# Six different starting bytes for the split weight buffers, and a 64-column gate tile

## The chip, the cores and the metric

The kernel runs on one core of one Trainium2 chip. The metric is the time of one execution on the device in microseconds (us), the median of the runs shown. Lower is better. Throughout, L298 means line 298 of the kernel before.

## The reference

The program is a chain of four transformer layers on one sequence of 512 tokens with 1024 features, all in float32: a layer with a gated linear memory (mLSTM) and a pooling branch, a layer with index-selected attention, a layer with window attention, and a layer with sparse attention in three branches. The last two are each followed by a feed-forward network of width 2816. What matters here is what the layers have in common: a dense product of the 512 tokens with a weight matrix from HBM.

```
def even_layer(x, g_norm, w_in, conv_w, b_if, g_head, w_pool, s_pool, w_out):
    xn = rmsnorm(x, g_norm)
    p = xn @ w_in
    q, k, v, o, z_a, gates, u, z_b = _split(p, EVEN_SPLITS)
    ...
    gates = gates + b_if
    i_pre, f_pre = gates[..., :A_HEADS], gates[..., A_HEADS:]      # 4 + 4 columns
    ...
    return x + jnp.concatenate([y_a, y_b], axis=-1) @ w_out

def swiglu(h, w_gu, w_down):
    gate, up = jnp.split(h @ w_gu, 2, axis=-1)
    return (jax.nn.silu(gate) * up) @ w_down
```

The gate projection has eight output columns: four input gates and four forget gates.

## The kernel before, in words

**Weights.** All weights pass through one ring of 281 chunks. A chunk is 128 partitions by eight blocks of 128 float32 columns (4096 bytes a partition), except for eight chunks of six blocks. The ring has three slots (`SLOTS = 3`). SyncE issues the load of chunk c + 3 into `raw` once the low part of chunk c has been made. ScalarE copies `raw` to `whi`, rounded to fp32r (`split_high`, L2390), two chunks ahead of TensorE. VectorE writes `wlo = raw - whi` (`split_low`, L2399). TensorE waits for `wlo` of its chunk.

**Products.** `Dense.products` (L289 to L301) makes one output tile of 128 features by 512 tokens: for each block of 128 input features it issues three fp32r matmuls into the same PSUM bank, low weights by high activations, high by low, and high by high. The weights are the stationary operand (128x128, 512 bytes a partition), the activations move (128x512). `DenseRows` (L412 to L414) and `DownRows` (L598 to L600) do it the other way round: 128 tokens are stationary and 512 weight columns move. A chunk of eight blocks is 24 matmuls in all three classes; one of six blocks is 18.

**Addresses.** Memory is handed out by `sb`, in steps of 32 bytes a partition. `line_up` (L2234) moves the next buffer to byte 128 of a 512-byte row; it stands ahead of `raw`, ahead of `xs` (the activations, high and low) and ahead of nearly every other operand of a matmul. `raw`, `whi` and `wlo` are one tensor each with the three slots inside. As a slot is 4096 bytes, each slot, and each 512-byte block of a slot, begins at byte 128 of a row; so does each tile of `xs`.

**The gate tile.** `e_gates` (L2607) is a `Dense` of one tile. Its chunk holds 32 weight columns from 5120 on and 96 from 5124 on, so that the four input gates come out at PSUM partitions 0 to 3 and the four forget gates at 32 to 35. The two steps of its eviction (L2604) read those eight partitions and no others. Its products are 24 matmuls.

**Order.** Each engine runs its own list of stages in program order; the chunks fix the order of the dense products, and other work (attention, memory, norms) is placed beside them or between them by hand. Nothing in the order is computed from addresses.

Of the kernel before, what the change touches and what calls it, by code (L numbers as in the profile page):

```python
# [23 lines left out]
F32R = mybir.dt.float32r  # L24
# [4 lines left out]
P = 128  # L29
# [20 lines left out]
SLOTS = 3  # L50
# [3 lines left out]
ROW, ROW_AT = 512, 128  # L54
# [78 lines left out]
class Dense(Stage):  # L133
# [2 lines left out]

    def __init__(self, k, name, x_hi, x_lo, steps, ready=None, readers=None, scale=None, beside=(), spread=None, evicted=None,
                 between=None, evict_first=False, lead=0, trail=None, trail_from=0, trail_free=None, second=True, scale_at=0,
                 halved=(), beside_first=(), split_last=False):
        self.trail_from, self.trail_free, self.split_last = trail_from, trail_free, split_last  # L140
        evict_first = evict_first or split_last
        self.second, self.scale_at, self.halved, self.beside_first = second, scale_at, halved, beside_first
        self.between, self.evict_first, self.lead, self.trail = between, evict_first, lead, trail
        self.k, self.name, self.x_hi, self.x_lo, self.steps = k, name, x_hi, x_lo, steps
        self.ready, self.scale, self.beside, self.spread, self.evicted = ready, scale, beside, spread, evicted
        spec = k.plan[k.planned]
        assert spec["name"] == name, (spec["name"], name)
        k.planned += 1
        self.sizes, self.together, self.first, self.last = spec["sizes"], spec["together"], spec["first"], spec["last"]
        self.tiles = spec["tiles"]  # L150
        self.tile0, self.bank0 = len(k.tile_steps), len(k.banked)
        self.first_step = k.steps_planned
        for n in range(self.tiles):
            count = len(steps(n))
            k.tile_steps.append((k.steps_planned, 1 if readers is None else readers(n), spec["units"][n]))
            k.steps_planned += count
        self.take_banks()
# [130 lines left out]

    def products(self, pe, c, j, part, n, blocks):  # L289
        k, nc, chunk = self.k, self.k.nc, self.k.chunks[c]  # L290
        out = k.banks[:, self.bank(n), :]
        for b in blocks:
            kt = sum(self.sizes[:part]) + b
            if n <= (1 if self.lead else 0) and self.ready is not None:
                self.ready(pe, kt)
            at = b * self.together + j
            first, last = kt == 0, kt == sum(self.sizes) - 1
            nc.tensor.matmul(out, k.wlo[:, chunk.slot, at, :], self.x_hi(kt), start=first, stop=False)  # L298
            nc.tensor.matmul(out, k.whi[:, chunk.slot, at, :], self.x_lo(kt), start=False, stop=False)  # L299
            ins = nc.tensor.matmul(out, k.whi[:, chunk.slot, at, :], self.x_hi(kt), start=False, stop=last)  # L300
        return ins  # L301

    def trail_pe(self, pe):
# [51 lines left out]
class DenseRows(Dense):  # L355
# [38 lines left out]
    def on_pe(self, pe):  # L394
        k, nc = self.k, self.k.nc
        low, summed, evac = k.sig("weights_low"), k.sig("tile_summed"), k.sig("tile_steps")
        for c in range(self.first, self.last):
            slot = k.chunks[c].slot
            g, part = divmod(c - self.first, 4)
            high, rest = [w[:, slot].rearrange("p (k t) c -> p k (t c)", k=2) for w in (k.whi, k.wlo)]  # L400
            pe.wait_ge(low.sem, CREDIT + c + 1)
            for t in range(QT):
                if part == 0 and g > 0:
                    before, readers, _ = k.tile_steps[self.tile0 + QT * (g - 1) + t]
                    pe.wait_ge(evac.sem, CREDIT + before + readers)
                if part == 0 and g == 0 and self.between is not None:
                    self.between(pe, t)
                out = k.banks[:, 4 + t, :]
                r = slice(t * P, (t + 1) * P)
                for b in range(2):  # L410
                    kt = 2 * part + b
                    nc.tensor.matmul(out, self.x_hi(kt)[:, r], rest[:, b, :], start=kt == 0, stop=False)  # L412
                    nc.tensor.matmul(out, self.x_hi(kt)[:, r], high[:, b, :], start=False, stop=False)  # L413
                    ins = nc.tensor.matmul(out, self.x_lo(kt)[:, r], high[:, b, :], start=False, stop=kt == MT - 1)  # L414
                if part == 3 or t == QT - 1:
                    ins.then_inc(summed.sem, 1)
            for b in self.beside:
                b.pe(pe, c - self.first)
# [145 lines left out]
class DownRows(Stage):  # L564
# [29 lines left out]
    def products(self, pe, c, t, h, signal=None):  # L594
        k, nc, kt = self.k, self.k.nc, c - self.first
        slot, r, out = k.chunks[c].slot, slice(t * P, (t + 1) * P), self.bank(t, h)
        high, low = [w[:, slot, 4 * h:4 * h + 4].rearrange("p a b -> p (a b)") for w in (k.whi, k.wlo)]
        nc.tensor.matmul(out, self.a_hi(kt)[:, r], low, start=kt == 0, stop=False)  # L598
        nc.tensor.matmul(out, self.a_lo(kt)[:, r], high, start=False, stop=False)  # L599
        ins = nc.tensor.matmul(out, self.a_hi(kt)[:, r], high, start=False, stop=c == self.last - 1)  # L600
        if signal is not None:
            ins.then_inc(signal.sem, 1)
# [1612 lines left out]
class Kernel:  # L2215
# [18 lines left out]
    def line_up(self):  # L2234

        self.room_used = (self.room_used + ROW - 1 - ROW_AT) // ROW * ROW + ROW_AT
        return self.room_used

    def sb(self, ctx, name, shape, dt=F32):

        at = self.room_used
        self.room_used += (4 * math.prod(shape[1:]) + 31) // 32 * 32
        assert self.room_used <= self.room_end, (name, self.room_used)

        def give_back():
            self.room_used = at
        ctx.callback(give_back)
        return self.place(name, shape, dt, at)
# [134 lines left out]
    def split_high(self, act, c):  # L2383
        if c >= len(self.chunks):
            return
        chunk = self.chunks[c]
        act.wait_ge(self.sig(f"weights_landed{chunk.slot}").sem, chunk.need)
        if c >= SLOTS:
            act.wait_ge(self.sig("tile_summed").sem, CREDIT + self.chunks[c - SLOTS].units)
        self.nc.scalar.activation(self.whi[:, chunk.slot, 0:chunk.blocks, :], self.raw[:, chunk.slot, 0:chunk.blocks, :],  # L2390
                                  ACT.Copy).then_inc(self.sig("weights_high").sem, 1)

    def split_low(self, dve, c):
        if c >= len(self.chunks):
            return
        chunk = self.chunks[c]
        dve.wait_ge(self.sig("weights_high").sem, CREDIT + c + 1)
        hi = self.whi[:, chunk.slot, 0:chunk.blocks, :]
        self.nc.vector.tensor_tensor(self.wlo[:, chunk.slot, 0:chunk.blocks, :], self.raw[:, chunk.slot, 0:chunk.blocks, :],  # L2399
                                     hi.bitcast(F32), ALU.subtract).then_inc(self.sig("weights_low").sem, 1)  # L2400

    def keep(self, dst, scale=None):
# [30 lines left out]
    def setup(self):  # L2433
        nc, d, ctx = self.nc, self.d, self.ctx
        tensor = lambda name, shape, dt=F32: self.sb(ctx, name, shape, dt)
        self.hT_at = self.room_used
        self.hT = tensor("hT", [P, MT, 512])
        self.ident = tensor("ident", [P, P])
        self.ones = tensor("ones", [P, P])
        self.line_up()  # L2440
        self.raw = tensor("raw", [P, SLOTS, 8, P])
        self.whi = tensor("whi", [P, SLOTS, 8, P], F32R)
        self.wlo = tensor("wlo", [P, SLOTS, 8, P], F32R)
        self.gains = tensor("gains", [P, 6, MT])
        self.xs_at = self.line_up()
        self.xs = tensor("xs", [P, 2, MT, 512], F32R)
        self.xs_hi, self.xs_lo = self.xs[:, 0], self.xs[:, 1]
        self.xtmp = tensor("x_tmp", [P, 2, 512])
        self.squares_at = self.room_used
        self.squares = tensor("squares", [P, 512])  # L2450
        self.rb = tensor("row_scale", [P, 512])
        self.weight_plan()
        for n in CREDITED:
            self.sig(n)
# [37 lines left out]
    def even(self):  # L2492
# [5 lines left out]
        with ExitStack() as c:  # L2498
# [104 lines left out]
            def gate_steps(n):  # L2603
                pre = lambda r, k: (lambda ps: nc.vector.tensor_tensor(gi[:, k, :], ps[r:r + 4, :], self.rb[r:r + 4, :], ALU.mult))  # L2604
                put = lambda k: (lambda ps: nc.scalar.activation(gi[:, k, :], gi[:, k, :], ACT.Identity, bias=bif[:, k:k + 1]))
                return [("dve", pre(0, 0)), ("dve", pre(32, 1)), ("act", put(0)), ("act", put(1))]
            e_gates = Dense(self, "e_gates", xh, xl, gate_steps, readers=lambda n: 2)  # L2607
            parts = [rows[:, i, :] for i in range(6)] + [rows2[:, i, :] for i in range(2)]
            gates = Gates(self, gi, parts, columns, everywhere, e_gates.done())
            pooling = Pooling(self, u, win, cnt, e_u.done(), even_loads)  # L2610
# [536 lines left out]
```

## Time and profile before

| | |
|---|---|
| Runs shown | 1933.13 and 1933.19 us, median 1933.16 us |
| Profiled execution, span from first to last instruction | 1933.0 us |
| PE busy | 1910.9 us (99%), 9688 matmuls |
| PEld busy (weight loads) | 1508.1 us (78%) |
| DVE, ACT, POOL busy | 1056.5 us (55%), 769.1 us (40%), 353.2 us (18%) |
| Granted TensorE clock | 0.998 of full speed (2.4 GHz) |
| DMA | mean 97 GB/s |

No other time of the profiled execution is given than its span. PE is the matmul part of TensorE and PEld its weight loads, which are shown as a separate row of work because they lie beside the matmuls. The duration of a matmul in the trace covers its way through the array and overlaps with the next one; what a matmul costs the stream is the distance from its start to the start of the next.

### The profile page before, as it was taken

Reading aid. Unit: us, or ns where it says so; the run is one execution under the profiler, and the core shown is the slowest. Engines: PE = TensorE matmul, PEld = TensorE weight load, DVE = VectorE, ACT = ScalarE, POOL = GpSimd, SP = SyncE. Lnnn points to the kernel's source line nnn. Section 1 sums busy time; section 2 is a strip of 40 time slices with the busy share of each in tenths; the row PEclk is TensorE's granted clock in tenths of the full one; section 3 lists DMA queues with packets and bytes.
Section 4 is the critical chain, followed back from the end, with each engine's and each line's share of the span. In section 5 each row is a group of like instructions: output and inputs, shape, how many; then the busy total and the mean of one; then the engine's idle time right before and its main releaser. Section 6 shows DMA issues by size and latency. Waiting matters only on the chain.

```text
span 1933.0 us, 25271 instructions
## 1 busy us (share of the span) xinstructions
PE 1910.9 (99%) x9688; PEld 1508.1 (78%) x9688; DVE 1056.5 (55%) x2005; ACT 769.1 (40%) x1407; POOL 353.2 (18%) x443
## 2 busy tenths in 40 slices
PE   9999999999999999999999999999999999999998
PEld 7887778888777668768888888888766788888886
DVE  4567644444699755475544443343777555444323
ACT  4343434433354554474322222232566442222213
POOL 0640000001130761062000000040266310000002
PEclk9999999999999999999999999999999999999999
DMA  9452324442423223313333333365100133333232
GB/s 206 133 174 66 101 89 149 152 142 76 111 66 88 76 56 87 93 50 88 98 99 98 98 93 99 92 182 170 36 2 2 45 98 98 100 97 99 99 98 77
DMA packets 297246, 187.67 MB, mean 97 GB/s; under 512 B 32543, under 2 KB 274719, under 8 KB 296870
## 3 DMA queue, kind: packets, MB, share of 16 engines
q1 hardware_dynamic: 288958, 168.02, 30.7%
q10 hardware_dynamic: 8168, 18.03, 2.4%
q8 instruction: 78, 1.28, 0.3%
q14 instruction: 42, 0.34, 0.1%
HBM read 183.79 MB, written 17.96 MB: 104 GB/s over the span
## 4 chain that ended last, share of the span: by engine, by line
PE 90%; DVE 6%; ACT 2%; issue 1%; DMA 1%; POOL 0%; ACTq 0%; SPq 0%; DVEq 0%
PE banks L298 21%; PE banks L299 21%; PE banks L300 21%; PE banks L2033 4%; PE banks L2002 4%; PE banks L2016 4%; PE banks L600 2%; PE banks L598 2%; PE banks L599 2%; PE banks L412 2%; PE banks L414 2%; PE banks L413 2%; PE banks L950 1%; DVE idx_score L1216 1%; PE banks L958 1%
## 5 line engine op out<-in xcount | busy, mean ns | idle before, releaser
L2399 DVE TENSOR_TENSOR wlo<-raw,whi 128x1024 fp32r<-128x1024 f32 (+1 forms) x281 | 361.5, 1288 | 322.7 <-ACT whi L2390 322.2
L298 PE MATMUL banks<-xs,wlo 128*128 128x512 f32 x1336 | 533.0, 399 | 0.1
L300 PE MATMUL banks<-xs,whi 128*128 128x512 f32 x1336 | 521.5, 390 | 0.0
L299 PE MATMUL banks<-xs,whi 128*128 128x512 f32 x1336 | 521.4, 390 | 0.0
L2390 ACT ACTIVATE whi<-raw 128x1024 fp32r<-128x1024 f32 (+1 forms) x281 | 293.1, 1045 | 248.7 <-PE banks L300 100.6
L298 PEld LDWEIGHTS banks<-xs,wlo 128*128 128x128 f32 x1336 | 251.3, 188 | 60.6 <-issue 7.4
L299 PEld LDWEIGHTS banks<-xs,whi 128*128 128x128 f32 x1336 | 251.5, 188 | 53.8 <-issue 3.3
L300 PEld LDWEIGHTS banks<-xs,whi 128*128 128x128 f32 x1336 | 251.3, 188 | 53.2
L524 POOL TENSOR_TENSOR squares<-squares,x_tmp 128x512 f32<-128x512 f32 x35 | 46.9, 1341 | 685.3 <-ACT x_tmp L516 685.3
L2128 POOL TENSOR_SCALAR prob<-prob,long_stat,gt_s 128x512 f32<-128x512 f32 (+3 forms) x128 | 76.5, 607 | 125.1 <-DVE long_stat L2076 125.1
L2963 ACT ACTIVATE a_hi<-ff_tmp 128x512 fp32r<-128x512 f32 x44 | 27.8, 632 | 166.1 <-DVE ff_tmp L2962 166.1
L2960 ACT ACTIVATE ff_tmp<-ff_tmp 128x512 f32<-128x512 f32 x44 | 27.8, 632 | 165.7 <-DVE ff_tmp L2959 165.7
L2164 ACT ACTIVATE prob<-prob,long_stat 128x512 f32<-128x512 f32 (+3 forms) x128 | 70.6, 552 | 40.3 <-DVE long_stat L2070 39.9
L2424 ACT ACTIVATE xs<-hT,gains 128x512 fp32r<-128x512 f32 x40 | 29.0, 724 | 134.2 <-DVE hT L2419 111.0
L2016 PEld LDWEIGHTS banks<-ident,prob 128*128 128x128 f32 x432 | 45.8, 140 | 40.5 <-issue 36.2
L412 PE MATMUL banks<-wlo,xs 128*128 128x512 f32 x192 | 75.1, 391 | 0.3 <-DVE wlo L2399 0.3
L678 POOL TENSOR_TENSOR tok_scaled<-tok,last_gain 128x512 f32<-128x512 f32 x8 | 10.3, 1286 | 353.6 <-DVE tok L656 353.6
L413 PE MATMUL banks<-whi,xs 128*128 128x512 f32 x192 | 74.8, 389 | 0.0
L414 PE MATMUL banks<-whi,xs 128*128 128x512 f32 x192 | 74.8, 389 | 0.0
L2962 DVE TENSOR_TENSOR ff_tmp<-banks,ff_tmp 128x512 f32<-128x512 f32 x44 | 30.4, 691 | 78.0 <-PE banks L300 78.0
L2959 DVE TENSOR_TENSOR ff_tmp<-banks,row_scale 128x512 f32<-128x512 f32 x44 | 30.4, 691 | 75.9 <-PE banks L300 75.8
L2016 PE MATMUL banks<-ident,prob 128*128 128x128 f32 x432 | 68.0, 285 | 2.1 <-ACT pT L2173 1.0
(402 smaller groups left out, 3217.6 us busy)
## 6 DMA issues: line engine op xcount, KB each, us to landing
raw<-in_ffn_w_gu SPq DMA_DIRECT2D x88, 512.0 KB, 3.8
raw<-in_e_w_in SPq DMA_DIRECT2D x56, 512.0 KB, 3.9
raw<-in_ffn_w_down SPq DMA_DIRECT2D x38, 512.0 KB, 3.5
s_skew<-s_bias ACTq DMA_DIRECT2D x6, 2560.0 KB
raw<-in_o_w_in SPq DMA_DIRECT2D x21, 512.0 KB, 4.0
raw<-in_e_w_out SPq DMA_DIRECT2D x16, 512.0 KB, 3.9
raw<-in_b_w_in SPq DMA_DIRECT2D x15, 512.0 KB, 3.9
raw<-in_a_w_qkv SPq DMA_DIRECT2D x10, 512.0 KB, 4.0
```

Source lines behind the costliest of these rows:

```text
L298: nc.tensor.matmul(out, k.wlo[:, chunk.slot, at, :], self.x_hi(kt), start=first, stop=False)
L299: nc.tensor.matmul(out, k.whi[:, chunk.slot, at, :], self.x_lo(kt), start=False, stop=False)
L300: ins = nc.tensor.matmul(out, k.whi[:, chunk.slot, at, :], self.x_hi(kt), start=False, stop=last)
L412: nc.tensor.matmul(out, self.x_hi(kt)[:, r], rest[:, b, :], start=kt == 0, stop=False)
L413: nc.tensor.matmul(out, self.x_hi(kt)[:, r], high[:, b, :], start=False, stop=False)
L414: ins = nc.tensor.matmul(out, self.x_lo(kt)[:, r], high[:, b, :], start=False, stop=kt == MT - 1)
L2002: ins = nc.tensor.matmul(S(s, x)[:, 0:nk], self.q[r, m, t * P:(t + 1) * P], self.key(e, m, x)[r, k0:k0 + nk], start=not masked, stop=True)
L2016: ins = nc.tensor.transpose(T[s % 2][0:r, (2 * b + x) * P:(2 * b + x + 1) * P], self.probs_of[s % 4][:, x, self.pad + b * P:self.pad + b * ...
L2033: ins = nc.tensor.matmul(self.O(s)[64 * x:64 * x + 64, :], self.value(e, m, x, kb, r), self.turned_of[s % 2][0:r, (2 * b + x) * P:(2 * b + ...
L2128: nc.gpsimd.tensor_scalar(pr, pr, self.st[:, s % 4, 2, x:x + 1], g, ALU.mult, ALU.mult).then_inc(self.ready.sem, 1)
L2390: self.nc.scalar.activation(self.whi[:, chunk.slot, 0:chunk.blocks, :], self.raw[:, chunk.slot, 0:chunk.blocks, :], ACT.Copy).then_inc(sel ...
L2399: self.nc.vector.tensor_tensor(self.wlo[:, chunk.slot, 0:chunk.blocks, :], self.raw[:, chunk.slot, 0:chunk.blocks, :], hi.bitcast(F32), AL ...
```

## The change

The two tensors `whi` and `wlo` of three slots become two lists of three tensors. Each is placed by a new function `part_at`, which moves to a given byte of a 512-byte row: the high buffers to bytes 128, 192 and 320, the low ones to bytes 384, 0 and 64. The padding this needs is 448 bytes a partition; the `line_up` ahead of `xs` still puts `xs` at byte 128 (one row of 512 bytes further on), and everything behind it keeps its byte in its row. `raw` doesn't move. `Dense` gets a parameter `cols`, which is 128 by default and 64 for the gate tile: its matmuls load 64 columns of the weights and write 64 PSUM partitions. The number, kind and order of the instructions, and all waits, stay as they are.

```
-                 halved=(), beside_first=(), split_last=False):
+                 halved=(), beside_first=(), split_last=False, cols=P):
+        self.cols = cols
...
-        out = k.banks[:, self.bank(n), :]
+        out = k.banks[0:self.cols, self.bank(n), :]
...
-            nc.tensor.matmul(out, k.wlo[:, chunk.slot, at, :], self.x_hi(kt), start=first, stop=False)
-            nc.tensor.matmul(out, k.whi[:, chunk.slot, at, :], self.x_lo(kt), start=False, stop=False)
-            ins = nc.tensor.matmul(out, k.whi[:, chunk.slot, at, :], self.x_hi(kt), start=False, stop=last)
+            nc.tensor.matmul(out, k.wlo[chunk.slot][:, at, 0:self.cols], self.x_hi(kt), start=first, stop=False)
+            nc.tensor.matmul(out, k.whi[chunk.slot][:, at, 0:self.cols], self.x_lo(kt), start=False, stop=False)
+            ins = nc.tensor.matmul(out, k.whi[chunk.slot][:, at, 0:self.cols], self.x_hi(kt), start=False, stop=last)
...
+    def part_at(self, name, at):
+
+        self.room_used = (self.room_used + ROW - 1 - at) // ROW * ROW + at
+        return self.sb(self.ctx, name, [P, 8, P], F32R)
...
-        self.whi = tensor("whi", [P, SLOTS, 8, P], F32R)
-        self.wlo = tensor("wlo", [P, SLOTS, 8, P], F32R)
+        self.whi = [self.part_at(f"whi{i}", at) for i, at in enumerate((128, 192, 320))]
+        self.wlo = [self.part_at(f"wlo{i}", at) for i, at in enumerate((384, 0, 64))]
...
-            e_gates = Dense(self, "e_gates", xh, xl, gate_steps, readers=lambda n: 2)
+            e_gates = Dense(self, "e_gates", xh, xl, gate_steps, readers=lambda n: 2, cols=64)
```

## Rows read from the trace of the kernel before

**Rows 1.** The page: spans, busy time, slices and the chain that ended last
```profile
span 1933.0 us, 25271 instructions
PE 1910.9 (99%) x9688; PEld 1508.1 (78%) x9688; DVE 1056.5 (55%) x2005; ACT 769.1 (40%) x1407; POOL 353.2 (18%) x443
...
PEclk9999999999999999999999999999999999999999
...
PE 90%; DVE 6%; ACT 2%; issue 1%; DMA 1%; POOL 0%; ACTq 0%; SPq 0%; DVEq 0%
```

**Rows 2.** Busy us and (xinstructions) of each engine in stretches; then clock, DMA share, GB/s
```profile
960.00:1120.00 160.00, 160.00 (x708) 132.58 (x707) 76.11 (x89) 45.91 (x58) 0.00 (x0) 1.00 0.33 97
1680.00:1800.00 120.00, 120.00 (x531) 99.42 (x530) 57.45 (x66) 34.82 (x44) 0.00 (x0) 1.00 0.33 97
1840.00:1880.00 40.00, 40.00 (x178) 33.15 (x177) 9.52 (x8) 7.43 (x7) 0.00 (x0) 1.00 0.30 92
```

**Rows 3.** Instructions in order of time (start us, duration us), all engines, first feed-forward network
```profile
1000.09 0.39 PE L298 MATMUL banks<-xs,wlo 128*128 128x512 f32 x1
1000.09 0.19 PEld L299 LDWEIGHTS banks<-xs,whi 128*128 128x128 f32 x1
...
1001.55 1.04 ACT L2390 ACTIVATE whi<-raw 128x1024 fp32r<-128x1024 f32 x1
...
1002.58 0.39 PE L300 MATMUL banks<-xs,whi 128*128 128x512 f32 x1
...
1002.63 1.23 DVE L2399 TENSOR_TENSOR wlo<-raw,whi 128x1024 fp32r<-128x1024 f32 x1 [0.26 <-ACT whi L2390]
...
1011.65 0.39 PE L298 MATMUL banks<-xs,wlo 128*128 128x512 f32 x1
```

**Rows 4.** The two lines that split the weights: duration ns min/median/max, first and last start
```profile
L2399 DVE TENSOR_TENSOR wlo<-raw,whi x281: 959/1226/3019, 6.2 to 1910.4; 128x1024 fp32r<-128x1024 f32 x137, 128x768 fp32r<-128x768 f32 x4
L2390 ACT ACTIVATE whi<-raw x281: 831/1046/1082, 5.1 to 1909.3; 128x1024 fp32r<-128x1024 f32 x137, 128x768 fp32r<-128x768 f32 x4
```

**Rows 5.** A plain float32 product, in order of time (start us, duration us)
```profile
230.24 1.02 PE L1051 MATMUL banks<-u,wp 128*128 128x512 f32 x2
231.10 1.02 PE L1051 MATMUL banks<-u,wp 128*128 128x512 f32 x2
```

**Rows 6.** PE in order of time, from the restart after a wait at 593.90 us
```profile
593.90 0.50 PE L298 MATMUL banks<-xs,wlo 128*128 128x512 f32 x1
594.24 0.40 PE L299 MATMUL banks<-xs,whi 128*128 128x512 f32 x1
594.48 0.40 PE L300 MATMUL banks<-xs,whi 128*128 128x512 f32 x1
...
596.56 0.39 PE L300 MATMUL banks<-xs,whi 128*128 128x512 f32 x1
```

**Rows 7.** A line with short matmuls: duration ns min/median/max, first and last start
```profile
L1752 PEld LDWEIGHTS banks<-key_blocks,qT_s x64: 187/192/193, 1341.6 to 1348.7; 128*128 128x128 f32 x64
```

**Rows 8.** Who waited for whom, longest in total (us in total, times, longest)
```profile
DVE wlo L2399 <- ACT whi L2390: 322.2, 220, 7.5
...
PE banks L412 <- DVE wlo L2399: 0.3, 1, 0.3
```

**Rows 9.** The end of the gate tile, in order of time, without weight loads
```profile
65.11 2.38 DVE L2399 TENSOR_TENSOR wlo<-raw,whi 128x1024 fp32r<-128x1024 f32 x1 [0.88 <-ACT whi L2390]
...
68.54 0.39 PE L300 MATMUL banks<-xs,whi 128*128 128x512 f32 x1
68.77 0.39 PE L412 MATMUL banks<-wlo,xs 128*128 128x512 f32 x1
68.97 1.40 DVE L2604 TENSOR_TENSOR gates<-banks,row_scale 4x512 f32<-4x512 f32 x2 [1.49 <-PE banks L300]
```

More of the change, by code:

```diff
@@ L399, in on_pe @@
             g, part = divmod(c - self.first, 4)
-            high, rest = [w[:, slot].rearrange("p (k t) c -> p k (t c)", k=2) for w in (k.whi, k.wlo)]
+            high, rest = [w[slot][:, :, :].rearrange("p (k t) c -> p k (t c)", k=2) for w in (k.whi, k.wlo)]
             pe.wait_ge(low.sem, CREDIT + c + 1)
@@ L596, in products @@
         slot, r, out = k.chunks[c].slot, slice(t * P, (t + 1) * P), self.bank(t, h)
-        high, low = [w[:, slot, 4 * h:4 * h + 4].rearrange("p a b -> p (a b)") for w in (k.whi, k.wlo)]
+        high, low = [w[slot][:, 4 * h:4 * h + 4].rearrange("p a b -> p (a b)") for w in (k.whi, k.wlo)]
         nc.tensor.matmul(out, self.a_hi(kt)[:, r], low, start=kt == 0, stop=False)
@@ L2389, in split_high @@
             act.wait_ge(self.sig("tile_summed").sem, CREDIT + self.chunks[c - SLOTS].units)
-        self.nc.scalar.activation(self.whi[:, chunk.slot, 0:chunk.blocks, :], self.raw[:, chunk.slot, 0:chunk.blocks, :],
+        self.nc.scalar.activation(self.whi[chunk.slot][:, 0:chunk.blocks, :], self.raw[:, chunk.slot, 0:chunk.blocks, :],
                                   ACT.Copy).then_inc(self.sig("weights_high").sem, 1)
@@ L2397, in split_low @@
         dve.wait_ge(self.sig("weights_high").sem, CREDIT + c + 1)
-        hi = self.whi[:, chunk.slot, 0:chunk.blocks, :]
-        self.nc.vector.tensor_tensor(self.wlo[:, chunk.slot, 0:chunk.blocks, :], self.raw[:, chunk.slot, 0:chunk.blocks, :],
+        hi = self.whi[chunk.slot][:, 0:chunk.blocks, :]
+        self.nc.vector.tensor_tensor(self.wlo[chunk.slot][:, 0:chunk.blocks, :], self.raw[:, chunk.slot, 0:chunk.blocks, :],
                                      hi.bitcast(F32), ALU.subtract).then_inc(self.sig("weights_low").sem, 1)
```

## The prediction

> **What bounds the kernel now.** I read the page first. TensorE is busy for 1910.9 of 1933.0 us, its clock is at full speed in all forty slices (2.4 GHz), and the chain that ended last runs through it for 90% of the span [rows 1]. No other engine comes near: VectorE has 55%, ScalarE 40%. So the question is what the changed addresses do to the rate of the matmuls, and whether anything they wait for gets late.
>
> The rate is in the table of busy time by stretch [rows 2]. In 160 us of the first feed-forward network 708 matmuls start, in 120 us of the second 531, in 40 us of the last product, where the weights move and the activations are stationary, 178: 226 ns each, a little under the true figure because the ends of the stretch are counted in. The order of time gives it more closely [rows 3]: from the matmul at 1000.09 us to the one at 1011.65 us there are 51 steps in 11.56 us, 226.7 ns a step. That is one number for all three classes of product, with `xs`, `a_hi` or the weights as the moving operand, and with both splits running at the same time (the ScalarE copy at 1001.55, the VectorE subtraction at 1002.63, in the same rows). 512 columns at 2.4 GHz are 213.3 ns, so each fp32r matmul pays 13.4 ns, 32 cycles, on top. That surcharge is the only thing in the profile that the addresses could touch at scale.
>
> How many matmuls are there to touch? 281 chunks [rows 4] of 24, less eight chunks that have 18: 281 x 24 - 8 x 6 = 6696. At 226.7 ns they are 1518 us, 79% of the span. One nanosecond on each is 6.7 us; 2% of the time (38.7 us, about what a measurement of this kernel can tell from no change) needs 5.8 ns on each.
>
> **The six bytes.** Removed and added instructions: none. What changes is the distance, within a row of 512 bytes, between what the weight load reads and what the matmul beside it streams. Before, it is zero everywhere: the load for the next matmul starts in the same hundredth of a microsecond as the matmul [rows 3], and both read from byte 128 on. After, the distances are 0, 64 and 192 for the high buffers and 256, -128 and -64 for the low ones. A high buffer serves two of three matmuls in a third of the chunks, so 2/9 of the 6696 each; a low one serves 1/9. The first high buffer stays at 128, so 7/9, 5208 matmuls, get a new distance.
>
> The trace of before shows no fp32r matmul at another distance, so the cost has to be bounded. From below: a plain float32 product (L1051) streams its 512 columns twice in each recorded matmul (16 matmuls in the code are 32 in the trace), and two of them take 0.86 us [rows 5], 430 ns each, 215 ns per 512 columns streamed, with weight loads beside it as well. If the surcharge came from both reads falling on the same place, and went, 226.7 - 215 = 11.7 ns would be saved on 5208 matmuls: 61 us. From above: after each restart the same matmuls run slower for about ten steps [rows 6]. From 594.24 to 596.56 us there are ten steps in 2.32 us, 232 ns on the average, the first of them 240. If that is what two unfavourably placed reads cost, 5208 matmuls lose between 5.3 and 13.3 ns: 28 to 69 us.
>
> I take zero. The reason is the steadiness: while a load reads 512 bytes, the matmul streams past the same 512-byte position more than once, since a weight load can follow the one before in (1348.7 - 1341.6) / 63 = 113 ns [rows 7], in which the stream covers 271 columns, 1084 bytes, two rows. Whatever the distance is, the two meet in every load. A fixed 32 cycles for 128 loaded columns looks like a price per load, not per meeting at a byte. And the slow steps after a restart happen with both reads at byte 128, so they need no address to explain them.
>
> The Trainium skill speaks against the change in its own way: SBUF — State Buffer, section "Who interferes with whom", says that TensorE has two independent read ports, one for the moving operand and one for the weight load, and that TensorE never waits on anyone. By it the sum would be exactly zero. The trace neither confirms nor refutes that, since all operands stand at one distance.
>
> **The splits.** The copy of ScalarE reads at byte 128 and now writes elsewhere, and VectorE reads `raw` and `whi` at different bytes. A copy takes 1.05 us and a subtraction 1.23 us [rows 4], together 2.27 us for each chunk, and a chunk lasts 24 x 226.7 ns = 5.44 us on TensorE. VectorE spends 322 us waiting for ScalarE in this chain, and TensorE waited for a low part for 0.3 us in the whole run [rows 8]. If each split took 10% longer, 0.23 us per chunk would vanish behind that. What would be late next, if the cover went, is the short stages with much beside work; the slowest subtraction there already takes 3.0 us [rows 4] and costs nothing that can be seen. Cost zero, ends zero and about 1 us.
>
> **The gate tile.** 24 matmuls still stream 512 columns each. Only their loads halve, and loads lie beside matmuls: 113 ns under 227 ns [rows 7, 2]. If the surcharge is a price per loaded column, half of 13.4 ns is saved 24 times: 0.16 us. The eviction starts 0.43 us after the start of the last of those matmuls [rows 9] and reads eight partitions as before; what follows on TensorE, the first product of `e_v`, doesn't wait for it. I book 0.2 us.
>
> **Sum.** 0 (bytes) + 0 (splits) - 0.2 (gate tile) against the span of 1933.0 us of the profiled execution, which lies 0.16 us below the median of the runs; so 1933.0 us on the scale of the runs. I put the number at 1932, since more small effects open downwards (a buffer that gets a little cheaper) than are excluded.
>
> **Rivals.**
> 1. **Faster: the surcharge is a meeting of two reads.** For it: the plain product at 215 ns, and that 13.4 ns is nearly the time in which 32 columns stream, a whole number. Against it: two rows pass per load, and the number is the same in all classes of product. If all five moved buffers get free of it: 1933 - 61 = 1872 us. If only the three low ones do: 3/9 x 6696 x 11.7 ns = 26 us, 1907 us. TensorE: Matmul & The Clock Gate, section "Back-to-back issue gap", gives N/2.4 + 2.5 ns for a warm matmul, 215.8 ns for 512 columns; the rows show 10.9 ns more, which that page doesn't explain. By that rule every matmul would save 10.9 ns if the change restored it, and the estimate would be 1860 us.
> 2. **Slower: the distance of zero was the good one.** The place is the weight load beside each matmul, in every stage, and the price is the one of the steps after a restart. For it: the slow steps exist, between 224 and 240 ns, and settle at 226.7, as two streams that find a good position would. Against it: they occur without any change of byte. All five moved buffers at 232 ns: 1933 + 28 = 1961 us; all at 240: 2002 us. It decides from 38.7 us / 5208 = 7.4 ns per matmul; its middle is near 1980 us.
> 3. **Mixed:** some buffers cheaper, some dearer, within 2%. One high buffer at 240 ns is 1488 x 13.3 ns = 20 us, one freed is 17 us less; so 1905 to 1960 us.
> 4. **The change doesn't do what it says.** The distances would stay zero if `xs` had moved with the buffers. It moves by a whole row, so this is excluded, and it gets no chance.
>
> **Chances.** Forecast, within about 3 us of 1932: 0.62. Mixed, inside 2%: 0.14. Faster by over 2%: 0.12. Slower by over 2%: 0.12. The range takes in the mixed case and the low end of the slower rival (1961), and the partial form of the faster one (1907): 1900 to 1964 us.
>
> **What would show it.** Right: in the same stretches of the feed-forward networks again 708 and 531 matmuls, matmul starts 226.7 ns apart whichever slot the chunk is in, and a gate tile with 128x64 loads whose steps are unchanged or 220 ns. Wrong: a step that differs by the slot (a pattern with a period of three chunks), or between the matmul beside a load of `wlo` and one beside a load of `whi`. If the steps after a restart change their sequence, addresses matter to TensorE's reads, and the steady rate will most likely have moved too. If VectorE's subtraction changes from 1.23 us while TensorE keeps its rate, the time stays as forecast. I would be most wrong if the 32 cycles go: nothing else in this kernel could move the time by more than 1%.

## The result: 0.9% slower, from the rate of the matmuls

The changed kernel takes 1949.67 us (1949.63 and 1949.71), the one before 1933.16 us: 16.5 us more, a ratio of 1.0086, interval 1.0056 to 1.0115. That is inside the stated range, but 17.7 us above the number of 1932, and it is a real change (the interval stays above 1) where the forecast was none.

The page of the changed kernel, beside [rows 1]:

```profile
span 1947.8 us, 25271 instructions
PE 1927.1 (99%) x9688; PEld 1506.0 (77%) x9688; DVE 1055.9 (54%) x2005; ACT 768.9 (39%) x1407; POOL 352.3 (18%) x443
...
PEclk9999999999999999999999999999999999999999
...
PE 92%; DVE 4%; ACT 2%; issue 1%; DMA 0%; POOL 0%; ACTq 0%; SPq 0%; DVEq 0%
```

As many instructions, the same clock, and VectorE, ScalarE and GpSimd as busy as before to within 1 us. TensorE alone is busy for 16.2 us more. The profiled execution of this kernel took 1949.63 us as a run, 1.8 us more than its span; later profiles of unchanged speed have the same 1.8 us (1931.5 of span to 1933.28). The span of 1933.0 us before therefore belonged to an execution about 1.6 us slower than the median, and its distance to the new span understates the change.

The busy time by stretch (columns as in [rows 2]) shows where it is:

```profile
960.00:1120.00 160.00, 160.00 (x698) 130.92 (x697) 75.64 (x87) 45.85 (x58) 0.00 (x0) 1.00 0.33 96
1850.00:1890.00 40.00, 40.00 (x176) 32.59 (x175) 8.57 (x7) 7.42 (x7) 0.00 (x0) 1.00 0.31 100
```

698 matmuls start where 708 did, and 176 where 178 did. The order of time tells more. These are the first matmuls of four chunks in a row (start us first), once in the first feed-forward network and once in the last product; the ring slots are 0, 1, 2 and 0 again. (In the changed kernel and all later ones these lines are numbered one higher, L299 for L298 of before.)

```profile
961.36 0.40 PE L299 MATMUL banks<-xs,wlo 128*128 128x512 f32 x1
...
966.83 0.40 PE L299 MATMUL banks<-xs,wlo 128*128 128x512 f32 x1
...
972.39 0.40 PE L299 MATMUL banks<-xs,wlo 128*128 128x512 f32 x1
...
977.89 0.40 PE L299 MATMUL banks<-xs,wlo 128*128 128x512 f32 x1
...
1846.44 0.40 PE L599 MATMUL banks<-wlo,a_hi 128*128 128x512 f32 x1
...
1851.90 0.40 PE L599 MATMUL banks<-wlo,a_hi 128*128 128x512 f32 x1
...
1857.45 0.39 PE L599 MATMUL banks<-wlo,a_hi 128*128 128x512 f32 x1
...
1863.05 0.40 PE L599 MATMUL banks<-wlo,a_hi 128*128 128x512 f32 x1
```

Divide the time from one line to the next by 24 matmuls, with the starts taken to the nanosecond. With stationary weights the slots take 227.8, 231.7 and 229.4 ns a step, with moving weights 227.5, 231.2 and 233.3; before, the chunks here had 226.7 [rows 3]. The step differs by slot, which is the sign that the prediction had named for being wrong. Within slot 0 the first four or five steps are slow (236, 229, 232, 231 ns) and the rest are 226.7 again; the other two slots settle into repeating patterns such as 229, 229, 236 and 226, 229, 232 ns.

The sum over a ring: (977.89 - 961.36) / 72 = 229.6 ns, 2.9 ns more than before, on the 5592 matmuls of `Dense`: 16.2 us. (1863.05 - 1846.44) / 72 = 230.7 ns, 4.0 ns more, on the other 1104: 4.4 us. Together 20.6 us, against 16.5 measured. Read over all starts in the trace, the steps below 260 ns carry 20.8 us above 226.7 ns, where before they carried 2.8: 18.0 us more, since the slow steps after a restart were there before. The longer steps, which hold waits, got about 2 us shorter (40.5 us in all, against 42.2 in the profile of `gate_only`, a kernel of unchanged speed shown below).

The weight loads of the gate tile took 134 ns instead of 188, as meant. Its 24 matmuls stepped at 228.7 ns.

### The profile page after: what moved, and what is told of

It reads as the page before. It is cut to its first block, busy times and chain, and to the rows that moved or that the text cites. A ratio compares the mean times of both kernels' runs of the same rounds, so it can differ in the third digit from the quotient of the medians.

```text
span 1947.8 us, 25271 instructions
## 1 busy us (share of the span) xinstructions
PE 1927.1 (99%) x9688; PEld 1506.0 (77%) x9688; DVE 1055.9 (54%) x2005; ACT 768.9 (39%) x1407; POOL 352.3 (18%) x443
## 4 chain that ended last, share of the span: by engine, by line
PE 92%; DVE 4%; ACT 2%; issue 1%; DMA 0%; POOL 0%; ACTq 0%; SPq 0%; DVEq 0%
PE banks L299 21%; PE banks L300 21%; PE banks L301 21%; PE banks L2034 4%; PE banks L2003 4%; PE banks L2017 4%; PE banks L413 2%; PE banks L415 2%; PE banks L414 2%; PE banks L601 2%; PE banks L600 2%; PE banks L599 2%; PE banks L951 1%; PE banks L959 1%; PE banks L1052 1%
## 5 line engine op out<-in xcount | busy, mean ns | idle before, releaser
L299 PE MATMUL banks<-xs,wlo 128*128 128x512 f32 x1336 | 533.9, 400 | 0.1
L299 PEld LDWEIGHTS banks<-xs,wlo 128*128 128x128 f32 x1336 | 250.5, 188 | 65.1 <-issue 7.6
```

Of the source, the lines that this page charges most:

```text
L299: nc.tensor.matmul(out, k.wlo[chunk.slot][:, at, 0:self.cols], self.x_hi(kt), start=first, stop=False)
```

## The experiments

All kernels are the changed one with other bytes, and in all but `gate_only` the gate tile has its 128 columns back. "Distance" is the byte of the weight buffer less the byte of the lined-up operand, within a row. A chunk's mean step is the time from its first matmul to that of the next chunk, divided by its matmuls.

### The gate tile alone, and the bytes alone

```
gate_only:   self.whi = ... enumerate((128, 128, 128))    self.wlo = ... enumerate((128, 128, 128))    (cols=64 stays)
bytes_only:  - e_gates = Dense(..., readers=lambda n: 2, cols=64)
             + e_gates = Dense(..., readers=lambda n: 2)
```

> All six weight buffers at byte 128 as before, the gate tile loads 64 columns. If the 16.5 us come from the bytes: within 0.3 us of before, steady step 226.7 ns in all chunks. If the narrow load does it (24 matmuls, and whatever state they leave behind): up to 1949.7 us, with slow steps from the gate tile on. If the surcharge of 32 cycles is a price per loaded column, the steps of the gate tile are 220 ns.

> Six bytes as in the change, the gate tile loads 128 columns. If the bytes are the cause: 1949.7 us, within 0.5 us of the changed kernel, with steady means of 226.7, 231.2 and 229.0 ns by slot in the feed-forward networks. If the gate tile is: 1933 us.

`gate_only`: 1933.12 us against 1933.12, ratio 1.0001 (0.9992 to 1.0010). `bytes_only`: 1949.71 us, ratio 1.0087 (1.0073 to 1.0101). The bytes are all of it. The steps by slot are those of the changed kernel. But the gate tile is no gain either. First matmul of the tile and first one behind it, in `gate_only`:

```profile
61.91 0.40 PE L299 MATMUL banks<-xs,wlo 128*64 128x512 f32 x1
...
67.43 0.39 PE L413 MATMUL banks<-wlo,xs 128*128 128x512 f32 x1
```

5.52 us for 24 matmuls, 230.0 ns each on the average, in a pattern of six steps (236, 229, 224, 227, 234, 230). With half the columns the matmuls are dearer by 3.3 ns, 0.08 us in all, which is too little to show in the time. A price per loaded column would have given 220 ns.

### One distance for all, and the same bytes for everything

```
all_192:      self.whi = ... enumerate((192, 192, 192))    self.wlo = ... enumerate((192, 192, 192))    (gate tile 128 columns)
rows_at_192:  as all_192, and  - ROW, ROW_AT = 512, 128   + ROW, ROW_AT = 512, 192
```

> All six weight buffers at byte 192, all other operands at 128: distance 64 everywhere, and no difference between one weight buffer and the next. Theory A (what counts is the distance between the weight load and the moving operand): every slot steady at 229 to 236 ns, 1933 + 6696 x 4.5 ns = about 1963 us. Theory B (what counts is the difference between one weight buffer and the next): steady 226.7 ns, 1933 us.

> Every lined-up operand and all six weight buffers at byte 192 instead of 128: distance zero, other absolute bytes. Theory A and theory B: 1933 us within 2 us (a few small operands ahead of the lined-up ones stay where they were). Theory C (a weight buffer must stand at byte 128, or 384, whatever the other operand does): as all_192, 1950 us or more.

`all_192` took 1970.47 us, ratio 1.0193 (1.0179 to 1.0206), dearer than the change itself and than the 1963 us expected. `rows_at_192`, with the same weight bytes but the other operands beside them, took 1933.27 us, ratio 1.0000 (0.9991 to 1.0010). First matmuls of two neighbouring chunks in `all_192`:

```profile
970.37 0.39 PE L299 MATMUL banks<-xs,wlo 128*128 128x512 f32 x1
...
975.97 0.39 PE L299 MATMUL banks<-xs,wlo 128*128 128x512 f32 x1
```

and in `rows_at_192`:

```profile
956.41 0.39 PE L299 MATMUL banks<-xs,wlo 128*128 128x512 f32 x1
...
961.86 0.39 PE L299 MATMUL banks<-xs,wlo 128*128 128x512 f32 x1
```

5.60 against 5.45 us a chunk: 233.3 against 227 ns (226.7 over three chunks). So a difference between one weight buffer and the next (theory B) isn't needed for the loss, and the absolute byte (theory C, here 192 against 128) isn't its cause. The distance between what is loaded and what is streamed is (theory A). A distance of 64 bytes costs 6.7 ns, 16 cycles, on top of the 32 that distance zero has.

The splits also read and write at changed bytes, and could be suspected. Between 900 and 1400 us of `all_192`, the 947 steps of these products that overlap a ScalarE copy or a VectorE subtraction of weights average 233.4 ns, and the 1090 that overlap none 233.3 ns (steps under 260 ns). So the extra time isn't made by the splits running beside.

### Only the low buffers moved

```
low_192:  self.whi = ... enumerate((128, 128, 128))    self.wlo = ... enumerate((192, 192, 192))
```

> High buffers at byte 128 (distance 0), low buffers at 192 (distance 64). Theory A, price paid by the matmul beside the load: in Dense only the matmul beside the load of the next low block (L301) pays, 6.7 ns every third step, mean 228.9 ns, 15 us in all, 1948 us. If the reads keep a state from one matmul to the next (the changed kernel's steps of slot 1, 229 229 236, did not fall on one matmul alone), the mean lies above that, up to 233.3 ns and 1970 us.

1958.14 us, ratio 1.0128 (1.0111 to 1.0145), between the two values expected. The order of time, four chunks from first to last:

```profile
965.08 0.40 PE L299 MATMUL banks<-xs,wlo 128*128 128x512 f32 x1
...
981.72 0.40 PE L299 MATMUL banks<-xs,wlo 128*128 128x512 f32 x1
```

16.64 us for 72 steps, 231.1 ns, where a price paid only beside the load of a low block would give 228.9. The steps repeat as 229, 229, 236 ns: the two matmuls beside loads at distance zero are 2 ns slower as well. A step depends on more than the load beside it, so the distances can't be priced one by one.

### The sweep

```
sweep_...:  self.whi and self.wlo at (128 + d0, 128 + d1, 128 + d2) mod 512, high and low of a slot at the same byte
             (in the last two kernels as views of one tensor, whi_wlo, since memory is handed out in steps of 32 bytes)
```

> High and low buffer of a slot at the same byte; the three slots at distance 32, 128 and 192 from the moving operand's byte 128. One look; the steady step in the second half of a chunk is read by slot. Theory A with a period of 256 bytes (slot 0 of the changed kernel had its low buffer at distance 256 and ran at 226.7 ns): distance 32 between 226.7 and 233.3 ns, about 230; distance 128 dearest, 233 ns or more; distance 192, being 64 short of 256, between 226.7 and 233 ns. Theory A with a period of 512: distance 192 as dear as 128.

> The same with distances 256, 320 and 384. Period 256: 226.7, 233.3 and the value of distance 128. Period 512: distance 256 is the farthest from zero and not 226.7 ns.

> The same with distances 448 (-64), 480 (-32) and 96. Period 256: distance 448 equals 192. If the cost is symmetric in the distance, 448 is 233.3 ns and 480 equals 32. A distance at which the step falls below 226.7 ns, towards 215 ns, would be the gain that rival 1 of the prediction named; none is expected by the reading that 32 cycles are a fixed price per load.

> High and low buffer of a slot at the same distance from the moving operand: 16, 224, 240 bytes in slots 0, 1, 2. If a distance below 32 bytes is harmless: 226.7 ns at 16 and 240. If every distance other than a multiple of 256 costs: above 229 ns at all three. A step below 226.7 ns anywhere would be a layout faster than before.

> The same with distances 4, 8 and 160 bytes. If units of 16 bytes are what meets: 226.7 ns at 4 and 8. If the exact byte counts: above 227 ns at 4 already. 160, between 128 (231.6 ns) and 192 (229.2 ns): 229 to 232 ns.

The five took 1962.32, 1957.52, 1964.87, 1951.52 and 1966.64 us, one run each. First matmuls of four chunks in `sweep_256_320_384` (distances 256, 320 and 384):

```profile
965.77 0.39 PE L299 MATMUL banks<-xs,wlo 128*128 128x512 f32 x1
...
971.21 0.40 PE L299 MATMUL banks<-xs,wlo 128*128 128x512 f32 x1
...
976.81 0.39 PE L299 MATMUL banks<-xs,wlo 128*128 128x512 f32 x1
...
982.38 0.39 PE L299 MATMUL banks<-xs,wlo 128*128 128x512 f32 x1
```

in `sweep_32_128_192`:

```profile
967.64 0.39 PE L299 MATMUL banks<-xs,wlo 128*128 128x512 f32 x1
...
973.23 0.39 PE L299 MATMUL banks<-xs,wlo 128*128 128x512 f32 x1
...
978.80 0.39 PE L299 MATMUL banks<-xs,wlo 128*128 128x512 f32 x1
...
984.30 0.39 PE L299 MATMUL banks<-xs,wlo 128*128 128x512 f32 x1
```

in `sweep_448_480_96`:

```profile
968.23 0.40 PE L299 MATMUL banks<-xs,wlo 128*128 128x512 f32 x1
...
973.73 0.40 PE L299 MATMUL banks<-xs,wlo 128*128 128x512 f32 x1
...
979.33 0.39 PE L299 MATMUL banks<-xs,wlo 128*128 128x512 f32 x1
...
984.94 0.40 PE L299 MATMUL banks<-xs,wlo 128*128 128x512 f32 x1
```

in `sweep_16_224_240`:

```profile
963.71 0.39 PE L299 MATMUL banks<-xs,whi_wlo 128*128 128x512 f32 x1
...
969.15 0.39 PE L299 MATMUL banks<-xs,whi_wlo 128*128 128x512 f32 x1
...
974.75 0.39 PE L299 MATMUL banks<-xs,whi_wlo 128*128 128x512 f32 x1
...
980.19 0.39 PE L299 MATMUL banks<-xs,whi_wlo 128*128 128x512 f32 x1
```

and of three chunks in `sweep_4_8_160`:

```profile
969.13 0.39 PE L299 MATMUL banks<-xs,whi_wlo 128*128 128x512 f32 x1
...
974.71 0.39 PE L299 MATMUL banks<-xs,whi_wlo 128*128 128x512 f32 x1
...
980.25 0.39 PE L299 MATMUL banks<-xs,whi_wlo 128*128 128x512 f32 x1
```

Divided by 24, for stationary weights (the starts taken to the nanosecond, one chunk for each value, with the first steps after the change of distance in it; 0 and 64 are from the kernel before and `all_192`):

| distance, bytes | 0 | 4 | 8 | 16 | 32 | 64 | 96 | 128 | 160 | 192 | 224 | 240 |
|---|---|---|---|---|---|---|---|---|---|---|---|---|
| ns a step | 226.7 | 232.5 | 231.0 | 227.0 | 233.0 | 233.3 | 233.8 | 231.8 | 233.2 | 229.3 | 233.0 | 226.7 |
| 256 bytes more | 226.7 | | | | | 233.2 | | 232.4 | | 229.4 | 233.2 | |

The period is 256 bytes: the second line repeats the first within 0.6 ns. It is not a smooth curve. 16 and 240 are as good as 0 in these chunks, 4 and 8 are not, and 192 is better than both its neighbours. Several expectations were wrong: 128 isn't the dearest, 32 (about 230 expected) and 160 (229 to 232) came out at 233, a distance and its negative don't cost the same (64 at 233.3, 448 at 229.4), and 4 and 8 aren't free although 16 is here. No distance is below 226.7 ns.

For 16 and 240 that is only half of what the run shows. Of the 51 chunks of slot 0 (distance 16) with stationary weights and no wait in them, 43 ran at up to 228 ns and eight at 232.9 to 233.4; of the 50 of slot 2 (distance 240), six ran at 229.1. All of these stand within a few chunks of a longer step of TensorE. One of the eight, from a chunk start to the next:

```profile
406.54 0.39 PE L299 MATMUL banks<-ya_c,whi_wlo 128*128 128x512 f32 x1
...
412.15 0.40 PE L299 MATMUL banks<-yb_e,whi_wlo 128*128 128x512 f32 x1
```

That is 233.4 ns a step at distance 16. Only distances 0 and 256 ran at 226.7 ns in all three classes of product, apart from the steps behind a wait or a change of distance.

The sign turns with the roles. Where the weights move (the last product), distance 320 ran at 229.6 ns and distance 192 at 233.1. Taken as load less stream these are 192 and 64 in the table, 229.3 and 233.3. The rule fails close to zero: slot 0 of `sweep_16_224_240` has load less stream 240 in the products with moving weights, and its 13 chunks without a wait there took 231.4 to 232.0 ns, not 226.7:

```profile
1848.21 0.40 PE L599 MATMUL banks<-whi_wlo,a_hi 128*128 128x512 f32 x1
...
1853.77 0.39 PE L599 MATMUL banks<-whi_wlo,a_hi 128*128 128x512 f32 x1
```

The step also depends on how a stretch is entered. In `all_192` the first product with moving weights ran at 228.9 ns, in the pattern 226, 229, 232, which is that of load less stream equal to 192:

```profile
74.23 0.39 PE L413 MATMUL banks<-wlo,xs 128*128 128x512 f32 x1
...
79.72 0.39 PE L413 MATMUL banks<-wlo,xs 128*128 128x512 f32 x1
```

while most later products of the same form in the same kernel ran at an even 233.3 ns. Distance 192 in `sweep_32_128_192` has both rates too: 229.3 ns in the chunk of the table, 233.3 in eight others with stationary weights. For one layout there can be two lasting patterns. That what came before picks one is a guess from where they occur; no run was made to test it.

### The period, checked by the time

```
period_256:  self.whi = ... enumerate((128, 384, 128))    self.wlo = ... enumerate((384, 128, 384))
```

> High buffers at bytes 128, 384, 128 and low ones at 384, 128, 384: distances of 0 and 256 only, high and low never at the same byte of a row of 512. If the period is 256 bytes: steady step 226.7 ns in every slot and product class, 1933.1 us, no difference from before. If slot 0 of the changed kernel was fast for another reason: any slot slower than 227 ns in its second half shows it.

1933.21 us, ratio 0.9997 (0.9988 to 1.0006), and 226.7 ns in every slot and class. Buffers at different bytes were free at distances of 0 and 256.

The table also gives back the changed kernel. Its slot 0 has distances 0 and 256, and runs at 226.7 ns once settled. Slot 2 has distance 192 modulo 256 in both its buffers: 229.4 ns measured, 229.3 in the table, and with moving weights 233.3 ns, the value of 64. Slot 1 mixes 64 and 384, and lies at 231.7.

### Narrow loads

```
narrow_loads:  all buffers at 128;  gu = Dense(self, f"ff_gu{layer}", ..., beside=beside, cols=(64, 32)[layer])
```

> All buffers at byte 128. The gate/up products of the first feed-forward network load 64 weight columns, those of the second 32; the other PSUM partitions keep old sums, so half and three quarters of the output features of these products are left out. If the 32 cycles are a price per loaded column: steps of 220 and 217 ns. If the step depends on how the load and the stream meet (the gate tile alone ran at 230 ns on the average with 64 columns): 230 ns with 64 columns, and with 32 columns open, 216 to 236 ns.

1941.39 us, one run, slower than before by 8 us. One chunk in each network, 64 columns and then 32:

```profile
955.46 0.40 PE L299 MATMUL banks<-xs,wlo 128*64 128x512 f32 x1
...
960.98 0.40 PE L299 MATMUL banks<-xs,wlo 128*64 128x512 f32 x1
...
1592.05 0.39 PE L299 MATMUL banks<-xs,wlo 128*32 128x512 f32 x1
...
1597.61 0.39 PE L299 MATMUL banks<-xs,wlo 128*32 128x512 f32 x1
```

230.0 and 231.7 ns. A quarter of the weights to load, and a dearer step. A price per column would have made the step shorter, and a fixed price per load would have left it, here and in `all_192`; the forecast leaned on such a price, and both forms are refuted. The narrow matmuls also write fewer PSUM partitions, so this run doesn't separate the shorter load from the narrower output.

## Why the prediction was wrong

**The count and the bounds** held. 6696 matmuls carry the change, and 5208 of them have a new distance. The range of 1900 to 1964 us holds the result, and the mixed rival (1905 to 1960 us, some buffers dearer, within 2%) comes nearest to what happened, except that none got cheaper; it had a chance of 0.14 against 0.62 for the forecast.

**The six bytes, booked at zero.** This is the step that failed. It said: whatever the distance is, load and stream meet in every load, so a fixed 32 cycles look like a price per load. The runs put three things in its place. The 32 cycles are not per column (`narrow_loads`). They are the whole surcharge only at distances 0 and 256 (the kernel before, `rows_at_192`, `period_256`), and at 16 and 240 in some chunks. Every other distance tried costs 2.6 to 7.1 ns more (the table), while `rows_at_192` shows that moving all operands together from byte 128 to 192 costs nothing. The evenness of 226.7 ns over three classes of product [rows 2, 3] was read as proof that nothing depends on addresses; but all these products stood at the one distance, zero. A number that never varies, in a trace where its supposed cause never varies, says nothing about that cause.

**The slow steps after a restart** [rows 6] were set aside as something that "need no address". They were the one sign in the trace that the step of these matmuls isn't fixed by their shape. Slot 0 of the changed kernel shows a similar run of steps (236, 229, 232, 231, 227; the restart of rows 6 ends in 235, 229, 233, 230, 227) at most changes of chunk, with no restart, where the chunk before stood at another distance. The upper bound made from them, 5.3 to 13.3 ns, was of the right size (`all_192` cost 6.7 ns in steady state), but that the slow steps after a restart and the price of a distance have one cause isn't shown, so the agreement may be luck. Rival 2 named the right condition, that zero was the good distance, and its low end (1961 us) missed by 11 us because slot 0 kept its rate although its low buffer stood at 256, and slot 2 came out at only 2.7 ns in `Dense`.

**Rival 1**, in which a new distance removes the 32 cycles, found no support: sixteen distances tried, none faster. The Trainium skill, TensorE: Matmul & The Clock Gate, section "Back-to-back issue gap", gives N/2.4 + 2.5 ns, 215.8 ns for 512 columns, as the gap of an isolated warm matmul, and about 131 ns for each of a stream of load and matmul pairs. The traces agree with neither: no chunk with fp32r operands averaged under 226.6 ns a step, and a quarter of the load didn't help.

**The ports.** SBUF — State Buffer, section "Who interferes with whom", in the Trainium skill gives TensorE two independent read ports and says that it never waits on anyone. For other engines the trace agrees: the steps are the same with ScalarE and VectorE splitting weights beside them [rows 3]. For TensorE's own two reads it doesn't: 16 cycles a matmul come and go with their distance alone (`all_192` against `rows_at_192`), so here the measurement decides. That they meet in the reads, and not elsewhere in TensorE, is argued from the addresses alone.

**The splits** were free, as booked: the median subtraction took 1.225 us after and 1.226 before [rows 4].

**The gate tile** was booked at a gain of 0.2 us and is a loss of 0.08 us by its steps in `gate_only`, neither of which the time can show.

**The number.** 1933.0 us was taken as a span that lies on the scale of the runs. Runs are 1.8 us longer than their spans, so it belonged to a slower execution; the median of the runs, 1933.16, makes the same sum, and nothing hung on it. The last step down to 1932 rested on small effects open downwards, and no run showed one.

What stays open: which of the two reads holds up the other, why 128 columns at a good distance settle at 32 cycles above the columns, why 64 and 32 columns settle higher, and what decides between two rates of one layout. The runs give the steps, not the mechanism inside TensorE.

## What to carry to other kernels

Where fp32r matmuls run back to back, put the stationary and the moving operand of each pair at the same byte of a 256-byte row, in every buffer of a ring, and exactly so: 4 bytes off cost 5.8 ns a step, and 16 bytes off were free only in some stretches; spreading buffers over different bytes cost 0.9% here, and one wrong byte for all of them 1.9%. When a stream of matmuls has a perfectly even step, look at what else is perfectly even before calling the step fixed, and read the irregular steps after restarts and at changes of buffer first. Loading 64 or 32 weight columns instead of 128 beside a stream of 512 saved nothing here; the step grew by 3.3 and 5.0 ns.

## What was not expected of the hardware

- The step of 512-column fp32r matmuls depends on load byte less stream byte, modulo 256: 226.7 ns at 0, 229.3 to 233.8 ns at the multiples of 32 (`sweep_` runs and `all_192`), and at 16 and 240 either near 226.7 ns or 229 to 233 ns in one and the same run.
- 4 bytes of distance cost as much as 32 do: 232.5 ns, and 237.6 ns in a chunk of the last product, where the weights move.
- A step of TensorE depends on the steps before it: patterns of three and more steps, several steps to settle after a change of distance, and two lasting rates (228.9 and 233.3 ns in `all_192`) for one layout.
- Fewer weight columns make the step longer: 226.7, 230.0 and 231.7 ns with 128, 64 and 32 columns.
- The plain float32 product takes 430 ns a recorded matmul [rows 5]. If that is two streams of 512 columns, as the prediction reads it, its surcharge is 1.7 ns a stream, not 13.4.
